# Down projection: second weight block loaded by GpSimd's queue before the residual's reloads, and 360 instead of 364 columns in the last chunk of the projections

## The reference

```python
h, sa, sk, sv, sc = hybrid_mixer(rmsnorm(yp, norm_mix[l]), ctx_a0, ctx_c0, None, None, *mix_w)
yp = yp + h
mk, mv = memory_kv(mem_prompt, norm_mem[l], w_xk[l], w_xv[l], xk_norm[l])
yp = yp + cross_attention(rmsnorm(yp, norm_x[l]), mk, mv, w_xq[l], xq_norm[l], w_xo[l])
yp = yp + sq_relu_mlp(rmsnorm(yp, norm_ff[l]), w_up[l], w_down[l])

def sq_relu_mlp(xn, w_up, w_down):
    return jnp.square(jax.nn.relu(xn @ w_up)) @ w_down
```

## Time and profile before

| | us |
|---|---|
| median of 3 runs | 1540.63 (1539.89 to 1541.21) |
| profiled execution, its own time | 1542.75 |
| its span, first to last instruction | 1541.0 |
| TensorE busy | 1521.9 (99%) |
| VectorE busy | 959.5 (62%) |
| ScalarE busy | 589.8 (38%) |
| GpSimd busy | 245.0 (16%) |
| DMA, mean rate | 123 GB/s |

### The profile page before, as it was taken

The page is one execution under the profiler, slowest core; times in us unless marked ns, Lnnn a source line. Parts: engine busy times, 40 slices in busy tenths (PEclk is TensorE's granted clock), DMA queues, the critical chain, the costliest instruction groups (busy, mean ns, idle before and its releaser), DMA issues.

```text
span 1541.0 us, 26647 instructions
## 1 busy us (share of the span) xinstructions
PE 1521.9 (99%) x10896; PEld 1447.4 (94%) x10896; DVE 959.5 (62%) x1348; ACT 589.8 (38%) x1015; POOL 245.0 (16%) x322
## 2 busy tenths in 40 slices
PE   8999999999999999999999999999999999999999
PEld 8999999997768999996799999999999999999999
DVE  7636777757678533446444896666665587647653
ACT  7421031146666222135422643334333333333332
POOL 1010000002100100000000054555444310010110
PEclk9999999999999999999999999999999999999999
DMA  8435111103100534012312244433354875354563
GB/s 279 140 108 169 49 42 42 45 1 113 57 29 28 179 122 152 28 52 77 98 73 84 84 157 157 150 144 128 128 185 164 309 235 193 103 189 124 178 214 106
DMA packets 64062, 189.32 MB, mean 123 GB/s; under 512 B 7888, under 2 KB 12040, under 8 KB 63808
## 3 DMA queue, kind: packets, MB, share of 16 engines
q1 hardware_dynamic: 39392, 95.30, 19.1%
q0 software_dynamic: 24560, 92.45, 16.7%
HBM read 138.58 MB, written 54.12 MB: 125 GB/s over the span
## 4 chain that ended last, share of the span: by engine, by line
PE 51%; DMA 4%; DVE 1%; ACT 0%; issue 0%; SPq 0%
PE ps L2776 20%; PE ps L2797 19%; PE ps L419 8%; DMA a<-wdn 3%; PE ps L2657 2%; PE ps L2629 2%; PE ps L2639 0%; DMA r_raw_a<-quads_d 0%; DVE B_lo L1954 0%; PE ps L472 0%; ACT B_hi L1304 0%; SPq L778 0%; ACT x_scores L1267 0%; DVE Y L2132 0%; DVE neg_max L1915 0%
## 5 line engine op out<-in xcount | busy, mean ns | idle before, releaser
L419 PE MATMUL ps<-A_hi,w_hi 128*128 128x364 f32 x768 | 172.4, 333 | 0.3 <-DVE Y L1523 0.3
L419 PE MATMUL ps<-A_hi,w_lo 128*128 128x364 f32 x768 | 169.4, 329 | 0.0
L419 PE MATMUL ps<-A_lo,w_hi 128*128 128x364 f32 x768 | 169.2, 328 | 0.0
L383 ACT ACTIVATE w_hi<-w_raw 128x1024 fp32r<-128x1024 f32 x42 | 44.3, 1059 | 289.7 <-PE ps L419 187.3
L419 PEld LDWEIGHTS ps<-A_hi,w_hi 128*128 128x128 f32 x768 | 131.6, 188 | 7.3 <-issue 6.5
L419 PEld LDWEIGHTS ps<-A_lo,w_hi 128*128 128x128 f32 x768 | 133.5, 188 | 0.0
L419 PEld LDWEIGHTS ps<-A_hi,w_lo 128*128 128x128 f32 x768 | 133.4, 188 | 0.0
L387 DVE TENSOR_TENSOR w_lo<-w_raw,w_hi 128x1024 fp32r<-128x1024 f32 x42 | 51.1, 1222 | 103.2 <-ACT w_hi L383 103.2
L2776 PE MATMUL ps<-t_hi,wq_hi 128*128 128x272 f32 x480 | 99.4, 288 | 0.3 <-issue 0.3
L2776 PE MATMUL ps<-t_lo,wq_hi 128*128 128x272 f32 x480 | 99.2, 288 | 0.0
L2776 PE MATMUL ps<-t_hi,wq_lo 128*128 128x272 f32 x480 | 99.1, 288 | 0.0
(11 more groups left out here) (315 smaller groups left out, 3557.4 us busy)
## 6 DMA issues: line engine op xcount, KB each, us to landing
w_raw<-slabs SPq DMA_DIRECT2D x67, 512.0 KB, 3.9
quads_d<-quad_sum POOLq DMA_DIRECT2D x64, 272.0 KB, 2.9
w_raw<-wdn POOLq DMA_DIRECT2D x32, 512.0 KB, 4.2
r_raw_a<-quads_d SPq DMA_DIRECT2D x56, 272.0 KB, 2.9
r_raw_b<-quads_d SPq DMA_DIRECT2D x56, 272.0 KB, 3.1
quads_d<-hid_stage POOLq DMA_DIRECT2D x48, 272.0 KB, 3.1
Y<-xT POOLq DMA_DIRECT2D x16, 546.0 KB, 5.0
y_d<-Y POOLq DMA_DIRECT2D x16, 546.0 KB, 3.2
```

The source lines that it names most:

```text
L383: e.activation(WH[:, par], RAW[:, par], ACT.Copy).then_inc(s.w_hi, 1)
L419: ins = e.matmul(PS[:, 3 * par + c, 0:CH], wt[:, wpar, w], xt[:, col:col + CH], start=(first and n == 0 and m == 0), stop=(last and n == l ...
```

## The change

There are three edits.

- The four loads of A21 leave SP's queue. POOL issues them after the first two stream pieces and ahead of the wait for the quads and the four residual reloads. Each still waits until the one before it has landed.
- The third chunk of each projection product is 360 columns wide in place of 364, in `pe_part` and `out_terms`.
- The four columns of banks 2 and 5 that are then not written are set to zero once, near the start, by two memsets on VectorE, and the counts of three waits for `pad_ready` go up by two.

```diff
@@ pe_part, and the same in out_terms
-                        ins = e.matmul(PS[:, 3 * par + c, 0:CH], wt[:, wpar, w], xt[:, col:col + CH],
+                        n_ = CH if c < NCH - 1 else CH - (T - TOK)
+                        ins = e.matmul(PS[:, 3 * par + c, 0:n_], wt[:, wpar, w], xt[:, col:col + n_],
@@ SP
-            def a21_load(z):
-                sp.wait_ge(s.prod, N_PROD)
-                if z:
-                    sp.wait_ge(s.a21_in, 16 * z)
-                sp.dma_start(ZA21[z][:, :, 0:512], wdn[W_A21 * KD + 4 * z:W_A21 * KD + 4 * z + 4]
-                             .rearrange("k p c -> p k c")).then_inc(s.a21_in, 16)
...
                 right_load(n)
-                if n in (9, 11, 13, 15):
-                    a21_load((n - 9) // 2)
@@ POOL
             g.wait_ge(s.sp_lo, N_PROD)
             stream_load(g, 0)
             stream_load(g, 1)
+            g.wait_ge(s.prod, N_PROD)
+            for z in range(4):
+                if z:
+                    g.wait_ge(s.a21_in, 16 * z)
+                g.dma_start(ZA21[z][:, :, 0:512], wdn[W_A21 * KD + 4 * z:W_A21 * KD + 4 * z + 4]
+                            .rearrange("k p c -> p k c")).then_inc(s.a21_in, 16)
             for q, v in ((s.b11_out, 16 * KD), (s.b21_out, 16 * KD), (s.b22_out, 16 * KD), (s.t_out0, 32 * KD),
@@ waits for pad_ready, three places
-                e.wait_ge(s.pad_ready, 9)
+                e.wait_ge(s.pad_ready, 11)
...
-                        e.wait_ge(s.pad_ready, 5)
+                        e.wait_ge(s.pad_ready, 7)
@@ VectorE, start
             e.memset(MIX[:, QT:QT + 1].bitcast(F32), 0.0).then_inc(s.sel_ready, 1)
+            for b_ in (2, 5):
+                e.memset(PS[:, b_, CH - (T - TOK):CH], 0.0).then_inc(s.pad_ready, 1)
```

More of the change, by code:

```diff
@@ L2551, in out_terms @@
                         col = k * T + c * CH
-                        e.matmul(PS[:, 3 * i + c, 0:CH], W2[wt][:, i, w], B[xt][:, col:col + CH],
+                        n_ = CH if c < NCH - 1 else CH - (T - TOK)
+                        e.matmul(PS[:, 3 * i + c, 0:n_], W2[wt][:, i, w], B[xt][:, col:col + n_],
                                  start=False, stop=False)
```

## The result

The change made the kernel slower: 1546.27 us in the median of 19 runs (the kernel before: 1541.39 in as many), a ratio of 1.0022 with a 95% interval of 1.0015 to 1.0029, or 3.4 us.

What follows compares the result with a forecast made beforehand. TensorE, busy 99% of the span, was taken to bound the kernel. Moving A21 (+0.7 us), 360 columns (-2.0) and memsets (nothing) gave -1.3 to -1.6, so 1539.2 us from a median of 1540.63; range 1533.8 to 1542.6.

Steps and rivals of the forecast that it cites:

- the residual comes too late: Rival: residual blocks land at 1250.3, step 16 starts at 1251.2 with lower clock behind; 1544.9 us, chance 0.12.
- What bounds the kernel, and the views read: Whole kernel: TensorE busy 99% of the span, so only matmul length, its waits and its clock can move the time.
- Right block 10 and the emptied queue: Down step 10: with A21 off SP, block 10 lands by about 1214, needed at 1222.5; 1.9 + 1.7 us gone.
- What is late next: Residual blocks on POOL, behind four megabytes, three waited for: landing at 1244.5 to 1245, a stall of 3.6 us at step 16.
- The gain of the removed stall: First 16 down steps: 4.6 us lost now, made of 1.9 at step 10, 1.0 end wait and 1.7 lower clock.
- edit 1: A21's loads moved from SP to POOL: 5.3 us lost where 4.6 were, +0.7 us, bounds -4.6 and +6.4.
- The clock behind the new stall: After step 16's wait: a stall of 3.6 us is followed by the lower clock, adding 1.7 us.
- Edit 2: Projections' third chunk at 360 columns: 1152 matmuls save 1.79 ns each, -2.0 us, bounds 1.8 and 2.1.
- Edit 3: Two memsets on VectorE near the start and higher wait counts: taken as nothing, memsets' bounds 0 and 0.2 us.

Runs made afterwards that it cites:

- without the chain: The changed kernel with A21's four loads issued at once, a semaphore for each, still ahead of the reloads: 1534.37 us, ratio 0.9954.
- The four profiled executions with A21 on SP: The kernel before, and it with a last chunk of 360, 352 or 362 columns: 660.8, 658.9, 656.7, 658.2 us from up projection to last down step.
- the other orders: The changed kernel with none, two or three of A21's four loads ahead of the residual reloads on POOL: ratios 0.9981, 0.9977, 0.9971.

## Why the prediction was wrong

The result lies outside the range (1533.8 to 1542.6) and on the slower side; the rival "the residual comes too late" came true, which had 0.12. Step by step:

- **What bounds the kernel, and the views read:** right. No profile shows the time moved by anything but TensorE's waits, its clock and the columns.
- **Right block 10 and the emptied queue:** right. No wait for a right block is left, the longest landing fell from 17.8 to 9.1 us, and without a stall step 15 ended at 1237.6, which is 1242.0 on the clock of before. The rule of the Trainium skill that issuing from several engines only saves issue time ("DMA: Bandwidth & Descriptors", section "Issuing engines are not separate DMA queues") does not cover this. The traces show more than issue time saved: without the chain some 7.5 MB went out on POOL within 7 us, the residual needed 19 to 23.5 us to land, and SP's right blocks, on the same 16 engines, at most 9.7.
- **What is late next:** the right mechanism, with its size near. In the version with the move alone the chained pieces took 6.8 and 6.1 us (forecast 6.4; in the changed kernel 7.3 and 6.2) and the last piece with the reloads 13.1 (13.1). The first piece took 12.1, and was forecast at 8.7 from a start 2 us later: landed at 1220.9, not 1219.5. The evacuation began at 1246.97, forecast 1244.5 to 1245. In the changed kernel it began at 1244.2, which is 1248.6 on the clock of before, since TensorE was 4.4 us ahead and the chain of landings only in part: POOL issued the first piece 1.8 us earlier than in the version with the move alone. I had let the columns shift everything alike; a chain of DMAs doesn't get shorter with them. The estimate of 4.4 us for a megabyte, from the Trainium skill ("DMA: Bandwidth & Descriptors", section "Anatomy of one DMA"), was too low beside right blocks and streams; the least that a profile shows for a piece of A21 is 5.6.
- **The gain of the removed stall** was the step that failed most, a little ahead of the late landing: 4.6 us in the sum, 2.0 to 2.4 by most of what was measured. I read 4.6 us from one execution and took it as what every run loses. Then I set the sum on the median, which lies 2.1 us below that very execution: those two don't go together. The four profiled executions with A21 on SP lose 2.4 us in the mean, and the timed runs say 2.0 (0.6 to 3.4) at 364 columns, though 4.8 (about 2.4 to 7.2) at 360. The 1.8 us wait at step 10 with the lowered clock behind it appeared in one of four executions. With 2.0 in place of 4.6, my own sum for edit 1 would have been +3.3; how far below 4.6 the true mean lies stays open.
- **The clock behind the new stall:** forecast 1.7 us. The changed kernel's 2304 matmuls after step 16's start took 292.43 us against 291.05, the move alone 292.40, so 1.4. But the long wait and the lower clock behind it are in both profiles with four chained pieces, and the mean clocks of their timed runs, 0.9961 and 0.9965, are the lowest of all timed versions; those with little or no wait have 0.9982 (364 columns, no chain) to 0.9996. The forecast set the same drop against the one of before as if both were in every run. The reading that a stall above 1.7 us brings the lower clock doesn't hold either: waits of 1.8 us (362 columns) and 2.4 us (360 columns alone) were not followed by it, one of 1.8 (before) and those of 3.2, 6.4 and 7.3 were.
- **Edit 2:** right in kind, mis-sized in the trace: 3.5 ns for each of 1152 matmuls, 4.0 us by that sum and 2.8 to 3.7 us by where the up projection begins, against 1.8 ns and 2.0 us. The step was the slope between 272 and 364 columns, used for the last four of 364; even its upper bound, 0.458 ns a column, was passed. In the timed runs it is 2.3 alone and 5.1 without the chain.
- **Edit 3:** no run tells it apart from edit 2, and no wait of TensorE near the start grew by more than 0.4 us.

With edit 1 at +6.6 for +0.7 and edit 2 at -2.3 to -4.0 for -2.0, the wrong sum is edit 1's. The profile of the move alone loses 7.9 us against a version without waits (664.1 for 656.2 from the up projection on), where I had 5.3: that is 2.6 of the 5.9 us that are missing, 2.2 of them the later landing (1246.97 for 1244.75). Some 2.2 more are the gain that wasn't there (2.4 for 4.6, by the four profiles). The last 1.1 us no profile places; they lie within the interval of the timed runs.

## What to carry to other kernels

When loads move to another queue, price what they now stand in front of: a load whose landing is waited for costs its size and its latency to everything behind it, while the DMA engines are not full (a share of 0.74 here, where 1.03 was reached without the waits); here four unchained megabytes in the same place turned 3.4 us of loss into 7.1 of gain. Two of the other orders fell short in the same way, by a wait that held later loads on the queue. And a stall of 2 us read in a single profiled execution may not be there in most runs: before it enters a sum, see whether what it waits for is late by much or only just, and compare the profiled run's clock and time with the others'.

## What the runs showed of the hardware

- The mean granted clock of a run orders the spans of one and the same kernel on average: 1537.2 us at 1.000 to 1542.0 at 0.996, though the four runs at 0.996 alone go from 1540.3 to 1543.7. The move alone, with a wait of 6.4 us, is 8.6 us slower than the version without the chain at the same 364 columns (1.0043 against 0.9987), and its mean clock is 0.9965 against 0.9982: a long stall costs more than its length. In the two profiles 7.6 of the 8.6 us are there, 1.4 of them as lower clock.
- The length of a short stall doesn't say whether the clock falls behind it: of two of 1.8 us one was followed by a stretch at the lower level, the other not, nor one of 2.4.
- Two queues share the engines far from first come, first served: 272 KB blocks on SP's queue landed within 9.7 us while 546 KB blocks issued in the same stretch on POOL's, behind four megabytes, needed up to 23.5.
- The price of a column of an fp32r matmul is uneven: 0.45 ns in the mean from 272 to 364 (125.6 and 166.7 ns a matmul), 0.87 from 360 to 364, 0.28 from 352 to 360.
